# Half-token pieces for the gate projection, and splits of weights behind the exponents, in a hybrid attention and SSD step

## What is computed

```python
proj = h @ p['w_in']
q, k, v, z, xbc, dt, gates = jnp.split(proj, SPLIT_IDX, axis=-1)
...
cb = jnp.einsum('bcign,bcjgn->bcgij', Cm, Bm)
y_diag = jnp.einsum('bcgij,bcgrij,bcjgr,bcjgrp->bcigrp', cb, decay, dt, x)
states = jnp.einsum('bcjgn,bcjgr,bcjgrp->bcgrpn', Bm, decay_to_end * dt, x)
...
y = rms_norm(y * jax.nn.silu(z), p['ssd_norm'])
merged = jax.nn.sigmoid(g_a) * (attn @ p['w_attn_o']) + jax.nn.sigmoid(g_b) * (y @ p['w_ssd_o'])
```

## Time and profile before

| | |
|---|---|
| median of 3 runs | 1854.9 us (1849.82 to 1855.33) |
| profiled execution | 1860.62 us, span 1858.9 us, mean granted TensorE clock 0.936 |
| busy, share of the span | TensorE 88%, VectorE 56%, ScalarE 36%, GpSimd 5% |
| chain that ended last | PE 72%, DVE 15%, ACT 7%, issue 3%, DMA 2% |
| context chunk | products at 520.6, group 7 ends at 579.0 us |
| products of latent chunks 1 to 4 | 662.2, 726.1, 790.5, 857.7 us |
| first scores of attention | 927.3 us |

### The profile page before, as it was taken

One profiled execution on the slowest core, in us unless ns is written; L12 is line 12 of the kernel. 1 busy time (PEld: TensorE's weight loads), 2 busy tenths in 40 slices (PEclk: granted clock), 3 DMA queues, 4 the chain that ended last, 5 costly groups with the idle time before them and its releaser, 6 DMA issues.

```text
span 1858.9 us, 27421 instructions
## 1 busy us (share of the span) xinstructions
PE 1638.2 (88%) x11141; PEld 1542.0 (83%) x11141; DVE 1031.8 (56%) x1419; ACT 662.4 (36%) x1099; POOL 99.5 (5%) x155
## 2 busy tenths in 40 slices
PE   4799999989998997888789899989289999999995
PEld 2699989889998987787755599989289999999995
DVE  5466675557754676786465353434934353342467
ACT  3544443334373265655455442321131121111210
POOL 1000012110101100000000000000000000000000
PEclk9799998999998999988899999999689999999998
DMA  9344355442486666664520164333102222223221
GB/s 306 98 128 139 126 172 195 131 136 65 153 268 235 211 208 222 179 205 163 181 106 23 46 199 148 115 139 112 45 24 69 70 74 71 79 68 90 68 68 56
DMA packets 159721, 241.14 MB, mean 130 GB/s; under 512 B 8048, under 2 KB 126560, under 8 KB 156576
## 3 DMA queue, kind: packets, MB, share of 16 engines
q1 hardware_dynamic: 136464, 171.45, 28.5%
q0 software_dynamic: 12304, 47.72, 6.9%
q10 hardware_dynamic: 10880, 20.97, 4.1%
HBM read 195.06 MB, written 45.06 MB: 129 GB/s over the span
## 4 chain that ended last, share of the span: by engine, by line
PE 72%; DVE 15%; ACT 7%; issue 3%; DMA 2%; SPq 0%; ACTq 0%; DVEq 0%
PE acc L805 64%; PE tp L805 5%; DVE arena L1850 2%; DVE wlo L1750 2%; ACT arena L1511 1%; ACT whi L1286 1%; PE tp L1190 1%; DVE arena L2003 1%; DMA arena<-in_w_mod 1%; PE tp L888 1%; DVE arena L1789 1%; DVE arena L1788 1%; ACT arena L1298 1%; DVE wlo L1801 1%; DVE arena L2005 1%
## 5 line engine op out<-in xcount | busy, mean ns | idle before, releaser
L805 PE MATMUL acc<-hh,whi 128*128 128x322 f32 x1408 | 343.3, 326 | 33.3 <-ACT arena L1298 20.1
L805 PE MATMUL acc<-hl,whi 128*128 128x322 f32 x1408 | 336.5, 321 | 0.0
L805 PE MATMUL acc<-hh,wlo 128*128 128x322 f32 x1408 | 333.2, 319 | 0.0
L805 PEld LDWEIGHTS acc<-hh,whi 128*128 128x128 f32 x1408 | 248.0, 199 | 37.1 <-ACT arena L1298 21.7
L805 PEld LDWEIGHTS acc<-hl,whi 128*128 128x128 f32 x1408 | 250.5, 198 | 0.0
L805 PEld LDWEIGHTS acc<-hh,wlo 128*128 128x128 f32 x1408 | 248.8, 197 | 0.0
L1286 ACT ACTIVATE whi<-raw 128x2048 fp32r<-128x2048 f32 x78 | 148.7, 1908 | 266.3 <-PE acc L805 266.3
L1750 DVE TENSOR_TENSOR wlo<-raw,whi 128x2048 fp32r<-128x2048 f32 x78 | 178.5, 2290 | 105.5 <-ACT whi L1286 105.2
L805 PE MATMUL acc<-whi,hh 128*128 128x256 f32 x720 | 207.6, 288 | 7.9 <-DVE hl L2238 7.9
L805 PE MATMUL acc<-whi,hl 128*128 128x256 f32 x720 | 204.3, 284 | 0.0
L805 PE MATMUL acc<-wlo,hh 128*128 128x256 f32 x720 | 204.1, 283 | 0.0
(11 more groups left out here) (255 smaller groups left out, 2331.3 us busy)
## 6 DMA issues: line engine op xcount, KB each, us to landing
raw<-in_w_in SPq DMA_DIRECT2D x38, 1024.0 KB, 7.0
raw<-in_w_mlp SPq DMA_DIRECT2D x32, 1024.0 KB, 5.4
arena<-in_w_mod SPq DMA_DIRECT2D x24, 1024.0 KB, 6.4
arena<-decay_sums_t ACTq DMA_DIRECT2D x40, 512.0 KB, 5.5
arena<-xs_nat SPq DMA_DIRECT2D x8, 1024.0 KB, 8.1
raw<-in_w_ssd_o SPq DMA_DIRECT2D x8, 1024.0 KB, 6.3
y_nat<-arena POOLq DMA_DIRECT2D x6, 1024.0 KB, 7.3
arena<-y_nat SPq DMA_DIRECT2D x6, 1024.0 KB, 5.9
```

Of the source, the lines that this page charges most:

```text
L805: return pe.matmul(out, l, r, start=first, stop=last)
```

## The change

1. A gate unit is still two pieces, but a piece (`gate_piece`) now does all 8 contraction steps of one half of the tokens, in one bank. It waits for the copy of the piece two back, and ScalarE copies each half (322 columns) by itself. POOL's store and the counts (`U_AO`) follow.
2. `F_LAT` and `F_LAT_G`: two pieces instead of three ahead of the products, two instead of one ahead of group 0, and the piece ahead of group 5 goes to group 6.
3. ScalarE's and VectorE's `weights` is parted in `results` and `splits`. In the scan's loops ScalarE does the splits after the exponents of the same group; those of group 7 come in the next chunk, on ScalarE behind exps of its group 0 and one square, on VectorE behind its first `scaled` and ahead of `masked`. In a group VectorE does the splits behind all results, before the weighting of the next group; in the context chunk its calls are otherwise as before.
4. `Z_STEPS`: the third and fourth block of z are fetched in groups 4 and 6 instead of 5 and 7, and SP's weight load of group 7 comes after the group's other loads.

```diff
@@ -331,7 +331,7 @@
         U_G = U_Z + DI // BW * NT
-        U_AO = U_G + 2 * 2 * D // BW
+        U_AO = U_G + 4 * 2 * D // BW
         U_SO = U_AO + KT
@@ -348,15 +348,15 @@
         F_CTX, F_CTX_G, F_H0, F_BACK = 4, [2, 2, 2, 2, 2, 2, 1, 1], 6, 1
-        F_LAT = [3, 3, 3, 3]
-        F_LAT_G = [1, 0, 1, 0, 1, 1, 0, 1]
+        F_LAT = [2, 2, 2, 2]
+        F_LAT_G = [2, 0, 1, 0, 1, 0, 1, 1]
         F_END = N_ZP + N_GP - (F_CTX + sum(F_CTX_G) + F_H0 + 12 * F_BACK + sum(F_LAT) + 4 * sum(F_LAT_G))
...
         Y_OUT = (1, 1, 2, 2, 3)
-        Z_STEPS = (1, 2, 5, 7)
+        Z_STEPS = (1, 2, 4, 6)
         GATED = {8 + 2 * q: q for q in range(4)}
@@ -532,7 +532,8 @@
                 for g in range(NG):
-                    weights(F_LAT_G[g])
+                    if g < NG - 1:
+                        weights(F_LAT_G[g])
                     if c + 1 < NT:
@@ -545,6 +546,7 @@
                         z_in(c, Z_STEPS.index(g))
+                weights(F_LAT_G[NG - 1])

@@ -748,7 +750,8 @@
                         u = (p - N_ZP) // 2
-                        po.wait_ge(free["sem"], due(free))
+                        step(free, 2)
+                        po.wait_ge(free["sem"], value(free))
                         po.dma_start(g_d[u], gst[:, u % 2]).then_inc(go[u % 2]["sem"], step(go[u % 2]))
@@ -1009,30 +1012,27 @@

-            def gate_half(n):
-
-                unit, part = n // 2, n % 2
+            def gate_piece(n):
+
+                unit, half = n // 2, n % 2
                 slot, sub = unit // 2 % 2, unit % 2
...
                     pe.wait_ge(lo["sem"], due(lo))
-                if part == 0:
-                    step(free)
-                    pe.wait_ge(free["sem"], value(free, 1))
-                for k in range(4 * part, 4 * part + 4):
+                step(free)
+                pe.wait_ge(free["sem"], value(free, 2))
+                for k in range(KT):
                     for w, m in ((whi, hh), (whi, hl), (wlo, hh)):
-                        for half in range(2):
-                            last = mul(acc[:, half, 0:HALF], w[:, slot, k, sub * P:(sub + 1) * P],
-                                       m[:, k, half * HALF:(half + 1) * HALF],
-                                       k == 0 and w is whi and m is hh, k == KT - 1 and w is wlo)
-                if part == 1:
-                    last.then_inc(ready["sem"], step(ready))
+                        last = mul(acc[:, half, 0:HALF], w[:, slot, k, sub * P:(sub + 1) * P],
+                                   m[:, k, half * HALF:(half + 1) * HALF],
+                                   k == 0 and w is whi and m is hh, k == KT - 1 and w is wlo)
+                last.then_inc(ready["sem"], step(ready))

...
                     else:
-                        gate_half(p - N_ZP)
+                        gate_piece(p - N_ZP)
                 step(pieces, n)
@@ -1471,10 +1471,9 @@

-            def weights(n):
+            def results(n):

                 for p in range(pieces["k"], pieces["k"] + n):
-                    b = block_done(p)
                     if p < N_ZP:
@@ -1482,17 +1481,30 @@
                         act.activation(zst[:, p % NT], acc[:, p % 2, 0:BW], ACT.Tanh, scale=0.5).then_inc(s["zt_ok"], 1)
-                    elif (p - N_ZP) % 2 == 1:
-                        u = (p - N_ZP) // 2
-                        if u == 0:
-                            for z in zo:
-                                act.wait_ge(z["sem"], value(z))
-                        step(go[u % 2])
-                        act.wait_ge(go[u % 2]["sem"], value(go[u % 2], 1))
-                        out_of_acc(gst[:, u % 2].rearrange("p (a b) -> p a b", a=2), acc[:, 0:2, 0:HALF], ACT.Copy)
+                    else:
+                        u, half = (p - N_ZP) // 2, p % 2
+                        if half == 0:
+                            if u == 0:
+                                for z in zo:
+                                    act.wait_ge(z["sem"], value(z))
+                            step(go[u % 2])
+                            act.wait_ge(go[u % 2]["sem"], value(go[u % 2], 1))
+                        out_of_acc(gst[:, u % 2, half * HALF:(half + 1) * HALF], acc[:, half, 0:HALF], ACT.Copy)
+                step(pieces, n)
+
+            split = count(s["acc_ready"])
+
+            def splits(n):
+
+                for p in range(split["k"], split["k"] + n):
+                    b = block_done(p)
                     if b is not None:
                         split_hi(b % 2)
-                step(pieces, n)
+                step(split, n)
+
+            def weights(n):
+                results(n)
+                splits(n)

@@ -1538,11 +1550,12 @@
             for g in range(NG):
-                weights(F_CTX_G[g])
+                results(F_CTX_G[g])
                 if g % 2 == 1:
...
                     exps(g + 2)
+                splits(F_CTX_G[g])
             weights(2)
@@ -1561,21 +1574,26 @@
             for c in range(1, NT):
-                weights(1)
+                results(1)
                 exps(NG * c)
...
                     squares(c - 1, 2, zq[:, 0])
-                weights(1)
+                    splits(F_LAT_G[NG - 1])
+                results(1)
                 exps(NG * c + 1)
...
                     squares(c - 1, 3, zq[:, 1])
-                weights(F_LAT[c - 1] - 2)
+                results(F_LAT[c - 1] - 2)
+                splits(F_LAT[c - 1])
                 for g in range(NG):
-                    weights(F_LAT_G[g])
+                    results(F_LAT_G[g])
                     if g + 2 < NG:
                         exps(NG * c + g + 2)
+                    if g < NG - 1:
+                        splits(F_LAT_G[g])
                     if g in (4, 6):
                         squares(c, g // 2 - 2, zq[:, g // 2 % 2])
+            splits(F_LAT_G[NG - 1])
             for q in (2, 3):
@@ -2099,12 +2128,16 @@
                 scaled(c, b, 0)
-                if c == 1:
-                    weights(F_LAT[c - 1])
+                if c > 1:
+                    splits(F_LAT_G[NG - 1])
+                results(F_LAT[c - 1])
                 masked()
+                splits(F_LAT[c - 1])
                 for g in range(NG):
                     weighted(g)
-                    weights(F_LAT_G[g] + (F_LAT[c - 1] if g == 0 and c > 1 else 0))
+                    results(F_LAT_G[g])
+                    if g < NG - 1:
+                        splits(F_LAT_G[g])
                     if g % 2 == 1:
```

## The result

| | before | changed | ratio, 95% interval |
|---|---|---|---|
| median of 4 runs each | 1855.1 us | 1877.7 us (1875.6 to 1883.1) | 1.0126 (1.0089 to 1.0163) |
| profiled execution | 1860.6 us | 1875.6 us | |
| its span | 1858.9 us | 1873.9 us | |
| granted TensorE clock, mean | 0.936 | 0.931 | |

The change made the kernel slower by 22.6 us by the medians and by 15.0 us in the two profiled executions: that of the changed kernel was the fastest of its four runs, that of the kernel before (1860.6 us) slower than the median of its own. The forecast was +20.6 us (1875.5 us, from 1864 to 1885).

A forecast was written before the change was run, and what follows sets the result against it. The prediction held that the order of work on ScalarE and VectorE, which TensorE waits behind, sets the time. Its terms summed to +20.6 us on a median of 1854.9 us, giving 1875.5 us, range 1864 to 1885.

The forecast's parts named there:

- The 10.1 us chain: From end of group g to start of g + 1: exponents, upper split, lower split, weighting and hops take 10.1 us.
- the predicted 4.6 and 4.4: Context chunk: the chain delays group 1 by 4.6 us and the group after group 2 by 4.4 us.
- Behind group 5, +7.6: Context chunk: state copies, scalings, skip and sum lengthen the chain; group 6 starts 6.4 us later, plus 1.2 us of clock.
- Clock in the context chunk, 2.5 a wait: Context chunk: each new wait after groups 0 and 2 brings a slow TensorE clock, costing 2.5 us.
- The h0 pieces, +1.1: Six pieces behind the context chunk: the lower split now follows all six results; about 1.1 of its 2.2 us shows.
- Chunk 1 +5.9: First latent chunk: wait between groups 0 and 1 grows 6.7 us, group 0 comes about 0.8 us earlier; +5.9 us.
- Turns: Latent chunk to chunk: chunk-end gain against longer group 0 to 1 gap; +1.0, +0.8 and -1.1 us.
- The last end, -8.7: End of the last latent chunk: gate-copy waits, slow clock behind them and a shorter last copy save 8.7 us.
- A: Rival: only the banks count, the splits' place costs nothing; chunk ends give -26.6 us, 1828 us; chance 0.07.
- B: Rival: the two sides cancel, something in the context chunk hides its three chains; -1.0 us, 1854 us; chance 0.05.
- C: Rival: 10 us waits keep the clock low through a second piece, 1.8 to 3.6 us at seven places; 1895 us; chance 0.10.

The follow-up runs named there:

- e1: Changed kernel with the context chunk put back: ScalarE splits weights ahead of the exponents of group g + 2 there; 1860.1 us.
- e2: Changed kernel with ScalarE's split of group 0 in the latent chunks put back ahead of the exponents of group 2; 1853.0 us.
- e5: Kernel before, with only ScalarE's splits of weights moved behind the exponents of group g + 2, in context and latent chunks; 1910.6 us.
- e3: Changed kernel with both split orders put back, in the context chunk and for group 0 of the latent chunks; 1832.6 us.
- e6: Kernel before with only the gate pieces of one bank each and their copies of 322 columns; 1842.4 us.
- e12: e3 with the piece tables of the kernel before (`F_LAT`, `F_LAT_G`); 1836.3 us.
- e7: e3 with VectorE's half of group 0's split in latent chunks moved behind group 7's weighted decays, its dependent load behind the chunk; 1820.4 us.

## Why the prediction was right

The forecast was the chain, with a chance of 0.78, and it came. Step by step, with the runs behind each (the figures of the changed kernel from its profiled execution):

- **The 10.1 us chain.** 10.2 us in all four latent chunks; 4.54 and 4.53 us of waiting in the context chunk for the predicted 4.6 and 4.4. e1 and e2 remove them by moving only the split, e5 makes them in the kernel before. The links as I listed them (3.95, 1.8, 2.2, 1.95 and 0.1) add up to 10.0, not 10.1; nothing hangs on it.
- **Behind group 5, +7.6.** The wait is 7.0 us at the states. Group 7 came 18.3 us after group 5 (577.58 to 595.92) for 11.8 before: +6.5.
- **Clock in the context chunk, 2.5 a wait.** From group 1 to group 2 took 11.2 us for 8.3, from 3 to 4 10.0 for 8.35: 2.8 and 1.7. The granted clock of TensorE over the 7.4 us behind the two waits was 0.60 and 0.77. The context chunk as a whole cost 20.2 us (h0 turn from the first products) for 21.6 predicted.
- **The h0 pieces, +1.1.** From the turn to the first back product took 17.7 us in both kernels. The 1.06 us wait is there, but the pieces ahead of it ran 1.3 us shorter. The waits ahead of the turn were alike (6.55 us before, 6.37 now), the clock behind them was not:

```profile
592.14:599.60 7.46, 7.46 (x41) 0.62 1.03 359
```

```profile
609.89:617.40 7.51, 7.51 (x53) 0.81 1.01 358
```

  The first row is the kernel before, the second the changed one. In the nine other kernels that have the 1.06 us wait, and whose context chunk keeps its speed (e1, e3, e6 to e12), the stretch is 18.5 to 19.0 us, 0.8 to 1.3 more than before: the term was right in size and hidden here.
- **Latent chunks.** Chunk 1 +5.9 (predicted +5.9). Turns +1.5, +0.7, -3.1 for +1.0, +0.8, -1.1. Only the third was mis-sized, by 2 us. I had charged that turn with what its end holds. In the kernel before a piece in the middle of it also ran slow, behind a wait of 1.8 us (5.06 us, at 834.04, for 3.81 in the chunk ahead), and cost 1.6 us that the sum left out. The changed kernel has such a piece as well (5.33 us, at 850.74), but there a later wait of 1.2 us went in exchange. In e5 the slow turn (73.7 us at a clock of 0.85) is the chunk before it. So that loss of clock does not belong to a certain chunk; what brings it on these runs do not settle.
- **The last end, -8.7.** -6.8 from group 1 of the last chunk to the first scores. Behind group 7 it is -9.0: the gate waits went as predicted. From group 1 to group 7 it is +2.2: the piece behind group 1 took 5.98 us for 4.89, and there is a new wait of 2.82 us for the decays of group 5. That wait is also in e3 (2.83), so the chain has no part in it; no run here settles where it comes from.

The measured terms sum to 20.2 + 5.9 + 1.5 + 0.7 - 3.1 - 6.8 = 18.4 us; the changed kernel's profiled execution was 2.5 us ahead when the scan began, which leaves 15.9, and the first scores came 16.0 us later. So the trace bears out 18.4 of the 20.6 us. That the total is so close owes something to luck: the terms above miss by up to 2 us each and in both directions, and the medians (+22.6) lie 2 us above the forecast where the trace's sum lies 2 us below it. One slip more: the forecast's own range, the clock terms at -6 and +2 with 3 us for the rest, comes to 1866.5 and 1880.5 us, not 1865 and 1882.

**The rivals.** A, only the banks count, gave 1828 us, and e3 shows that as a size it was right (1832.6) once the splits are back; as a mechanism it was half right, since the banks alone give -16 and moving group 7's split alone -14. I had priced the two as one thing. B, the context chunk hides its chains: it hid nothing. C, a longer wait keeps the clock low for longer: TensorE alone behind the 10.24 us wait (length, busy, clock, DMA share, GB/s) shows 0.57 over 7.6 us, where the earlier trace rows had 0.59 over 7.4 us behind the wait of 3.49 us that ended at 738.59.

```profile
698.42:706.00 7.58, 7.58 (x33) 0.57 0.88 309
```

The pieces right behind the four groups 1 took 5.99, 5.80, 5.68 and 5.98 us for 5.27, 5.75, 5.96 and 4.89 before, 0.4 us more on average. The next piece ran at full speed in all four chunks (3.8 us), so C, which asked for 1.8 to 3.6 us at each place, did not come. The Trainium skill ("TensorE: Matmul & The Clock Gate", What's actually happening) puts the ramp, said there of a kernel's warm-up, at under 1% of a typical kernel span. The clock lost behind two waits in the context chunk, 4.5 us, agrees with that as a share of the kernel (0.24%), and is still a fifth of the difference between these two kernels: for a comparison of two kernels 1% apart it has to be counted.

## What to carry to other kernels

When a step is split between two engines, do not move the first half back and leave its partner where it was: a partner that waits in order for the moved half stops everything queued behind it, and the price is the length of the whole new chain, not that of the step. The second half alone can go later at no such price (e7 gained 12 us by it). Ask of each such step when its result is first needed; here the weights of group 0 were wanted only after group 7, and the best place was neither the old one nor the new. Test the parts of a mixed change apart: this one held a gain of 25 us and a loss of 48.

## What the runs showed of the hardware that was not expected

The clock behind a wait does not follow from the wait's length alone. Over the 7.5 us behind the four waits of 10.24 us the granted clock was 0.56 to 0.61, the 1.2 GHz level for most of it; behind four waits of 3.35 to 4.35 us in the kernel before it was 0.56 to 0.72, and behind two waits alike, 6.55 and 6.37 us, 0.62 and 0.81. A wait three times as long cost hardly more clock, and two of one length can differ by more than 1 us. And the same instructions in latent chunks of the same kernel can take 70.4 or 73.7 us (e5), with VectorE and ScalarE busy for the same 48 and 37 us and a clock of 0.89 or 0.85: a single turn of a chunk is not a clean measure of a change below 3 us.
